# Last feed-forward of a two-block transformer kernel: first product by seven block products on halves of 256 tokens

## The reference, cut to what matters

```
D_FF_2 = 2816
def swiglu(h, w1, w2):
    a, b = jnp.split(h @ w1, 2, axis=-1)     # w1: 1024 x 5632
    return (jax.nn.silu(a) * b) @ w2         # w2: 2816 x 1024
def ffn_sublayer(x, m, i, g, w1, w2):
    return x + HALF_STEP * m[:, 3 * i + 2, None] * swiglu(mod_norm(x, m, i, g), w1, w2)
```

## Time and profile before

| | us |
|---|---|
| median of 3 runs | 3350.95 |
| lowest, highest | 3350.13, 3354.4 |
| profiled execution | 3347.27 |
| its span | 3345.5 |
| TensorE busy | 3238.1 (97%) |
| VectorE busy | 2444.6 (73%) |
| ScalarE busy | 1278.2 (38%) |
| GpSimd busy | 627.0 (19%) |

### The profile page before, as it was taken

The page is one execution under the profiler, slowest core; times in us unless marked ns, Lnnn a source line. Parts: engine busy times, 40 slices in busy tenths (PEclk is TensorE's granted clock), DMA queues, the critical chain, the costliest instruction groups (busy, mean ns, idle before and its releaser), DMA issues. The chain is left out here.

```text
span 3345.5 us, 45701 instructions
## 1 busy us (share of the span) xinstructions
PE 3238.1 (97%) x18042; PEld 2877.2 (86%) x18042; DVE 2444.6 (73%) x4483; ACT 1278.2 (38%) x2257; POOL 627.0 (19%) x657
## 2 busy tenths in 40 slices
PE   7989999999999999999999999999999999999998
PEld 6788778888999998877799999989999978788887
DVE  5576578888898898576788889888877865753333
ACT  4475543333332234345533333443333343533222
POOL 0100011112522221301052222143222213100000
PEclk9999999999999999999999999999999999999999
DMA  5201245554233333533213433322333243123332
GB/s 176 64 20 51 77 158 184 170 188 142 67 119 115 104 105 98 154 95 85 73 57 104 126 107 111 95 76 86 120 114 117 91 122 94 49 83 98 96 99 78
DMA packets 381928, 348.89 MB, mean 104 GB/s; under 512 B 17440, under 2 KB 338336, under 8 KB 381200
## 3 DMA queue, kind: packets, MB, share of 16 engines
q1 hardware_dynamic: 337696, 250.74, 24.8%
q0 software_dynamic: 17232, 46.84, 4.7%
q10 hardware_dynamic: 26784, 48.37, 4.5%
HBM read 339.60 MB, written 2.10 MB: 102 GB/s over the span
## 5 line engine op out<-in xcount | busy, mean ns | idle before, releaser
L824 PE MATMUL ps<-Hh,hib 128*128 128x512 f32 (+2 forms) x2672 | 955.9, 358 | 12.2 <-DVE Hl L2516 5.9
L824 PE MATMUL ps<-Hl,hib 128*128 128x512 f32 (+2 forms) x2672 | 946.0, 354 | 0.0
L824 PE MATMUL ps<-Hh,lob 128*128 128x512 f32 (+2 forms) x2672 | 945.7, 354 | 0.0
L1608 ACT ACTIVATE hib<-rawb 128x1024 fp32r<-128x1024 f32 (+2 forms) x589 | 508.9, 873 | 607.7 <-PE ps L824 606.8
L2381 DVE TENSOR_TENSOR lob<-rawb,hib 128x1024 fp32r<-128x1024 f32 (+2 forms) x361 | 441.4, 1226 | 383.7 <-ACT hib L1608 381.7
L824 PEld LDWEIGHTS ps<-Hh,hib 128*128 128x128 f32 x2672 | 507.8, 190 | 74.0 <-DVE Hl L2516 11.0
L824 PEld LDWEIGHTS ps<-Hh,lob 128*128 128x128 f32 x2672 | 507.6, 190 | 52.3
L824 PEld LDWEIGHTS ps<-Hl,hib 128*128 128x128 f32 x2672 | 508.3, 190 | 49.7 <-issue 1.0
L824 PE MATMUL ps<-Gha,hib 128*128 128x512 f32 (+1 forms) x704 | 238.0, 338 | 3.0 <-DVE lob L2381 1.9
L824 PE MATMUL ps<-Gla,hib 128*128 128x512 f32 (+1 forms) x704 | 237.3, 337 | 0.0
L824 PE MATMUL ps<-Gha,lob 128*128 128x512 f32 (+1 forms) x704 | 236.7, 336 | 0.0
(11 more groups left out here) (330 smaller groups left out, 5759.4 us busy)
## 6 DMA issues: line engine op xcount, KB each, us to landing
rawb<-in_ffn_w_in SPq DMA_DIRECT2D x114, 512.0 KB, 3.9
rawb<-in_ffn_w_out SPq DMA_DIRECT2D x76, 512.0 KB, 3.4
rawb<-in_w_in SPq DMA_DIRECT2D x74, 512.0 KB, 3.7
rawb<-in_w_ff SPq DMA_DIRECT2D x64, 512.0 KB, 3.8
rawb<-in_ffn_w_in SPq DMA_DIRECT2D x124, 256.0 KB, 3.3
MRa<-in_w_mod_t ACTq DMA_DIRECT2D x117, 256.0 KB, 3.3
MR<-in_w_mod_t POOLq DMA_DIRECT2D x112, 256.0 KB, 3.5
MRb<-in_w_mod_t ACTq DMA_DIRECT2D x59, 256.0 KB, 3.2
```

The costliest lines, as they stand in the source:

```text
L824: return e.matmul(out, lhsT, rhs, start=start, stop=stop)
L1608: return e.activation(out, src, f, **k)
```

## The change

Pairs 3 to 21 of the last feed-forward are computed by seven products, over halves of 256 tokens; pairs 0 to 2 stay plain. The parts are 3, 8 and 11 pairs, so the second product has three rounds of sweeps and not two. It has no seam there (`N != ("b", 1)`). The activation sums, their buffers and GpSimd's work are made for this feed-forward too. The matrix sizes of all others stay as they were.

```
-HALF = 384
+HALVES = {("a", 0): 384, ("b", 0): 384, ("a", 1): 384, ("b", 1): 256}
-def crossed(j, l):
-    return (j, l) != ("b", 1)
 def parts_of(j, l):
-    sizes = (PLAIN, 4, 4, 4, 3, 4) if crossed(j, l) else (11, 11)
+    sizes = (PLAIN, 8, 11) if (j, l) == ("b", 1) else (PLAIN, 4, 4, 4, 3, 4)
     return [(sum(sizes[:n]), sizes[n]) for n in range(len(sizes))]
...
             for f in range(f0, f0 + many):
-                if crossed(*name) and f >= PLAIN:
+                if f >= PLAIN:
                     cross((name, "in", f), w1, [128 * f, FF2 + 128 * f])
...
-                for n in "hl" if crossed(j, l) else "":
-                    sb(f"pad{n}{j}{l}", [128, 3, T + TC], where=s4)
-                    T2[j, l].append(sb(f"T{n}{j}{l}", [128, 2, HALF], where=s4))
+                for n in "hl":
+                    sb(f"pad{n}{j}{l}", [128, 2 * half * PLAIN], where=s4)
+                    T2[j, l].append(sb(f"T{n}{j}{l}", [128, 2, half], where=s4))
+                    if many > PLAIN + 1:
+                        sb(f"rest{n}{j}{l}", [128, 2 * half * (many - PLAIN - 1)], where=s4)
...
-        def acts_block(H_, b, q):
-            t0 = HALF * ((b - 1) // 2)
-            return H_[:, 2 * q + (b - 1) % 2, t0:t0 + HALF]
+        def acts_block(N, H_, b, q):
+            half = HALVES[N]
+            t0 = half * ((b - 1) // 2)
+            return H_[:, 2 * q + (b - 1) % 2, t0:t0 + half]
...
 (tensor: ffn)
-                        if crossed(*N) and f >= PLAIN:
+                        if f >= PLAIN:
                             seven(N, name)
...
                     residual((N, "out", part_), sets, ga, following(l, i) if part_ == len(parts) - 1 and len(sets) == 2 else None,
-                             crossed(*N))
+                             N != ("b", 1))
...
 (scalar: ffn)
-                if crossed(j, l):
-                    in_turn(grouped([lambda m=m, q=q: acts_sums(N, m, q) for m, q in SUMS], SUMS_BY))
+                in_turn(grouped([lambda m=m, q=q: acts_sums(N, m, q) for m, q in SUMS], SUMS_BY))
...
 (vector: ffn)
-                if crossed(j, l):
-                    in_turn(acts_sums(N))
+                in_turn(acts_sums(N))
...
 (gpsimd)
             def ffn(j, l, i):
                 N = (j, l)
-                name = {"x": xnorm(l, i), "c": cnorm(l, i)}
+                name = {"x": xnorm(l, i), "c": cnorm(l, i)} if (j, l) != ("b", 1) else {"x": xnorm(l, i)}
...
                 if l == 0:
                     load(mod_silu[TURNS["b", 0]], d["cc_rows"], "cc", TURNS["b", 0])
-                    ffn("b", l, 2)
+                ffn("b", l, 2)
                 fence(("b", l))
```

More of the change, by code:

```diff
@@ L620, in program @@
             for j in "ab":
-                many = max(n for _, n in parts_of(j, l))
+                many, half = max(n for _, n in parts_of(j, l)), HALVES[j, l]
                 s4 = ExitStack()
                 T2[j, l] = []
-                for n in "hl" if crossed(j, l) else "":
-                    sb(f"pad{n}{j}{l}", [128, 3, T + TC], where=s4)
-                    T2[j, l].append(sb(f"T{n}{j}{l}", [128, 2, HALF], where=s4))
+                for n in "hl":
[3 more added lines that the diff above has]
+                        sb(f"rest{n}{j}{l}", [128, 2 * half * (many - PLAIN - 1)], where=s4)
                 s4.close()
                 s4 = ExitStack()
-                G2[j, l] = [sb(f"G{n}{j}{l}", [128, many, T + TC], F32R, where=s4) for n in "hl"]
-                if crossed(j, l):
-                    E2[j, l] = [sb(f"E{n}{j}{l}", [128, 3, 4, HALF], F32R, where=s4) for n in "hl"]
-                    SUM2[j, l] = sb(f"SUM{j}{l}", [128, 3, 512], where=s4)
+                G2[j, l] = [sb(f"G{n}{j}{l}", [128, many, 2 * half], F32R, where=s4) for n in "hl"]
+                E2[j, l] = [sb(f"E{n}{j}{l}", [128, 3, 4, half], F32R, where=s4) for n in "hl"]
+                SUM2[j, l] = sb(f"SUM{j}{l}", [128, 3, 512], where=s4)
                 if (j, l) in TURNS:
@@ L722, in acts_sum @@
                 return E2[N][half][:, (5, 6, 7).index(m), q, :]
-            return acts_block(H_, 3 if m == 3 else ACTS[m][0], q)
+            return acts_block(N, H_, 3 if m == 3 else ACTS[m][0], q)
         def scratch(N, half, m, q):
@@ L730, in acts_operand @@
         def acts_operand(N, half, which, q):
-            return acts_sum(N, half, int(which), q) if isinstance(which, str) else acts_block((Hh, Hl)[half], which, q)
+            return acts_sum(N, half, int(which), q) if isinstance(which, str) else acts_block(N, (Hh, Hl)[half], which, q)
         def raw_of(c):
@@ L2116, in seven @@
             def seven(N, name, part, f, last):
+                half = HALVES[N]
                 def slot(which):
-                    return Tm[:, get("tmp", "seven", name, which)[0], 0:HALF]
+                    return Tm[:, get("tmp", "seven", name, which)[0], 0:half]
                 def gate(which):
@@ L2128, in high @@
                     w.wait_ge(*at("gfree", N, part - 1))
-                    act(G2[N][0][:, f, HALF * t:HALF * t + HALF], slot(which), ACT.Copy).then_inc(*done(("ghi", name, t)))
+                    act(G2[N][0][:, f, half * t:half * t + half], slot(which), ACT.Copy).then_inc(*done(("ghi", name, t)))
                 for pos, x in enumerate(P[name].units):
@@ L2141, in seven @@
                         w.wait_ge(*at("full", name, 1))
-                        act(slot("u"), ps[:, bank("o", name, 1), 0:HALF], ACT.Copy).then_inc(
+                        act(slot("u"), ps[:, bank("o", name, 1), 0:half], ACT.Copy).then_inc(
                             *done(("free", "o", name, 1), ("copied", name)))
@@ L2164, in ffn @@
                         name = (N, "in", f)
-                        if crossed(j, l) and f >= PLAIN:
+                        if f >= PLAIN:
                             seven(N, name, part, f - f0, f == f0 + many - 1)
@@ L3013, in seven @@
             def seven(N, name, part, f, last):
+                half = HALVES[N]
                 def slot(which):
-                    return Tm[:, get("tmp", "seven", name, which)[0], 0:HALF]
+                    return Tm[:, get("tmp", "seven", name, which)[0], 0:half]
                 def product(m):
                     w.wait_ge(*at("full", name, m))
-                    return ps[:, bank("o", name, m), 0:HALF]
+                    return ps[:, bank("o", name, m), 0:half]
                 def add(to, a, b, *keys, op=ALU.add):
@@ L3030, in low @@
                     w.wait_ge(*at("ghi", name, t))
-                    t0 = HALF * t
-                    e.tensor_tensor(G2[N][1][:, f, t0:t0 + HALF], slot(a), G2[N][0][:, f, t0:t0 + HALF], ALU.subtract).then_inc(
+                    t0 = half * t
+                    e.tensor_tensor(G2[N][1][:, f, t0:t0 + half], slot(a), G2[N][0][:, f, t0:t0 + half], ALU.subtract).then_inc(
                         *done(("tmp", "seven", name, a), *keys))
@@ L3425, in acts_sums @@
                     for k in (2 * q, 2 * q + 1):
-                        for s in "xc":
+                        for s in name:
                             w.wait_ge(*at("h", name[s], k))
```

6 lines of the change are left out of this document (3 added, 3 removed).

## The result

| | before | after |
|---|---|---|
| median, us | 3350.54 (4 runs, 3348.66 to 3354.4) | 3391.3 (4 runs, 3386.44 to 3392.23) |
| ratio, 95% interval | | 1.0117 (1.01 to 1.0135) |
| profiled execution, us | 3347.27 | 3392.23 |
| its span, us | 3345.5 | 3390.4 |

The changed kernel is slower by 1.2%, some 41 us. The forecast was 3354.0 with a range up to 3372; the time lies outside it, beyond the rival on VectorE's queue (3375) too.

What follows compares the result with a forecast made beforehand. A loop through the raw weight buffers, 11.5 us a pair, was taken to bound the pairs by seven; -15.2 + 12.9 + 1.6 + 0.4 + 2.5 + 0.8 = +3.0 us gave 3354.0 us, range 3342 to 3372.

Steps and rivals of the forecast that it cites:

- rival on VectorE's queue: Pairs by seven: VectorE's in-order queue sets the pace, 12.3 us a pair; +24 us, 3375; chance 0.18.
- matmuls, 19 x 0.80: TensorE, 19 pairs: 10.08 us by seven products against 10.88 plain, saving 0.80 a pair, 15.2 us.
- waiting in the two parts: Parts of 8 and 11: TensorE waits as pairs fall behind from the third on, 4.3 + 8.6 = 12.9 us.
- three plain pairs: Opening plain pairs: activation sums delay the fifth weight chunk, TensorE waits 1.6 us (0 to 4).
- round for the part of 3, clock included: Second product, part of 3: 2.5 us waiting for the third pair's G, plus 0.8 for lower clock.
- norm: Final norm: GpSimd's first two sums meet its last steps on SBUF operands, 0.4 us (0 to 1).
- a loop through the raw weight buffers: Pairs by seven: fourth sum, load and next three sums set 11.5 us a pair (10.8 to 12.2); chance 0.62 with the stalls.
- VectorE's own need: VectorE in a pair by seven: 11.0 us, scaled from 12.3 at 384 columns, above TensorE's 10.08.
- second rival: Pairs by seven: VectorE's queue decides, including 1.3 us of unhidden waits, less 2 x 4 done ahead; 3375, chance 0.18.
- The remark on the fourth sum: GpSimd's fourth sum: its 3.84 us wait for VectorE's low halves left out, as these come earlier at 256 columns.
- third rival: TensorE's clock: waits of 1.5 us in every pair bring it down, five falls of 1.7 us; +11.5, 3362; chance 0.06.
- The place of the waits: Last pairs of each part: TensorE would wait at m=6, behind a low half of SUM.

Runs made afterwards that it cites:

- e_nosum: Changed kernel with GpSimd's four weight sums in the last feed-forward cut to 8 of 128 columns, part of the computation left out; ratio to before 0.9996.
- e_sum4: Changed kernel with two places in turn for the fourth sum of weights in the last feed-forward; ratio to before 1.0117, stage 398.2 us.
- e_raw4: Changed kernel with a fourth raw weight buffer from the last plain pair of the last feed-forward on; ratio to before 1.0125, stage 402.2 us.
- e_both: Changed kernel with interleaved first sweeps in the part of 3, two places for the fourth sum and a fourth raw buffer; ratio to before 1.0141, stage 407.9 us.
- e_seam: Changed kernel with the two first sweeps of the part of 3 interleaved; ratio to before 1.0117, stage 399.4 us.
- e_fulld: Changed kernel with second gating one product later, interleaved first sweeps, fourth raw buffer and two places for the fourth sum; median 3380.72 us, ratio to before 1.0101.
- e_defer: Changed kernel with each pair's second gating and what hangs on it one product later on VectorE and ScalarE; median 3372.8 us, ratio to before 1.0072.

## Why the prediction was wrong

| step | predicted, us | measured, us |
|---|---|---|
| matmuls, 19 x 0.80 | -15.2 | -15.2 at the pace of 0.120 (e_nosum, 10.1 a pair) |
| waiting in the two parts | +12.9 | +47.3 |
| three plain pairs | +1.6 | +1.6 |
| round for the part of 3, clock included | +3.3 | +8.4 |
| other rounds | 0 | +0.3 |
| norm | +0.4 | not separable from where the stage starts |
| sum | +3.0 | +42.5 on the stage |

**The step that failed** is the one that set what bounds a pair: "the tighter thing is a loop through the raw weight buffers", 11.5 us. Of 42.5 us on the stage, freeing one of its buffers took 5.1 or 1.1 (e_sum4, e_raw4), and freeing both, with the seam, added 4.6 (e_both). What binds is VectorE's queue, with what it loses beside GpSimd's sums and waiting for ScalarE. It was already in the loop that I read from the earlier trace rows. The 1.65 us from the end of the fourth sum (2635.37) to the load (2637.02) I took for a fixed step of SyncE's, but the load went out 0.03 us behind a low half of VectorE's (start us, us; kernel before):

```profile
2636.31 0.68 DVE L2383 TENSOR_TENSOR lob<-rawb,hib 128x512 fp32r<-128x512 f32 x1
```

So did every load of the changed kernel's part of 11. Nor was the loop's range all above a plain pair's 10.88, as the prediction says: its lower end was 10.8.

VectorE's own need I had at 11.0 us from "12.3 - 11 x 0.12" and put aside as below the loop. It was 12.2: 8.0 us of work and 4.2 of standing behind GpSimd's sums (e_nosum beside the changed kernel). The subtraction is right for the work, but it keeps the standing as it was at 384 columns. In four pairs there (2087.30 to 2145.40) the operations with both inputs in SBUF lasted 9.5 us longer than 0.68 and 0.548 us each, 2.4 a pair:

```profile
L2383 DVE TENSOR_TENSOR lob<-rawb,hib 128x512 fp32r<-128x512 f32 x14 | 16.6, 1193 | 0.7 <-ACT hib L1608 0.6
...
L3023 DVE TENSOR_TENSOR Tm<-Tm 128x384 f32<-128x384 f32 x7 | 4.9, 694 | 0.1
L3032 DVE TENSOR_TENSOR Glb<-Tm,Ghb 128x384 fp32r<-128x384 f32 x6 | 4.6, 762 | 0.0
```

In the pair shown above it is 3.9, so the same four sums held VectorE up for some 1.5 us more. To this comes the time in which VectorE waits for ScalarE behind its own gating, 1.43 us a pair, which I had only in the second rival, as 1.3. The second rival had the mechanism and the right side, and its 12.3 us was too small for a pair at 13.6; its slack of 4 us in each part was too small the other way (11 x 13.61 - 139.0 = 10.7 in the part of 11).

**The remark on the fourth sum failed too.** I let its 3.84 us of waiting in the earlier trace rows go, since those low halves "hang on TensorE's pace and come earlier at 256 columns". They hang on VectorE's queue, and the fourth sum still waits 2.3 us in eleven of the 19 pairs and 0.1 to 0.9 in the others.

**A term was left out.** At the start of the second product after a part by seven, TensorE waits 1.6 us for the first weight chunk's low half: 2 x 1.6 = 3.2 of the 47.3 (L2380 in the list of waits).

**The part of 3.** Its place was right, the third pair's G behind the sum m = 3. It was mis-sized: 5.3 us of waiting for 2.5, and for the clock 3.0 for 0.8 (4 us at 0.50 and 6 at 0.83, 2.0 + 1.0 lost). By these shares TensorE ran for 6 us at half clock; the third rival's 1.7 us for such a fall and the 3.4 us at half clock in the expectation of e_seam were too low. I had only the chain of one pair, and not the low half and the addition in front of it in VectorE's queue.

**What was right.** The pace of the matmuls, and that the first pairs of a part keep 10.1 us. The plain stage's 1.6 came out in part by luck: the wait was 0.9 us, and 0.4 of the rest lies in the first pair, ahead of that wait. The place of the waits was wrong: I had them in front of product 6, behind its sum, and they are in front of 4, 3 and 1. In the part of 11 the first pairs took 27.22 us for 2.7 pairs' matmuls with no wait at all; such a stretch by itself would have borne out the forecast, and the loss comes only after it.

The third rival, the clock, held in one place only: 0.50 after the gap of 5.3 us. In the parts by seven, with waits of up to 1.7 us in every pair from the third on, the granted clock stayed at 1.00.

Open is why e_raw4 and e_sum4 by themselves differ by 4 us. VectorE is busy for 47.5 us in four pairs of the one and 45.6 in four of the other (3220.00 to 3273.24, 3220.57 to 3272.15), which is the right size, but why its operations meet the sums differently was not followed up.

## What to carry to other kernels

Where VectorE and GpSimd share a stage, split VectorE's busy time into work and time behind GpSimd, by comparing the mean of the same operation with and without a sum beside it; only the first part scales with the tile, and the second has to be reckoned anew (2.4 us a pair at 384 columns, 3.9 here). On an engine that runs in order the waits inside its queue cost as much as its work, so moving a gating and what hangs on it back in two queues (-20 us on the stage) can be worth more than two more buffers (+5 us, the seam's gain in it). Before a gap between two events is taken for a latency, see what ended it. And when a cheaper method loads a helper engine, use it for as many steps as that engine can follow, with the old method between them.

## What the runs showed of the hardware that I had not expected

- Freed buffers can cost time: the fourth sum started earlier and cost VectorE 0.86 us a pair that the wait had hidden (e_fulld beside e_defer; read from the traces, not isolated).
- A load on SyncE's queue follows what releases it closely: 0.03 us behind VectorE's low half, in the earlier trace rows and throughout the part of 11.
- GpSimd's sums hardly suffer in this meeting: 1.30, 1.35 and 1.62 us with VectorE operations beside them, 1.28 to 1.71 in the earlier trace rows, though one of the 76 in the changed kernel took 2.15. It is VectorE that stands, three operations in a row. No run shows a full sum with VectorE quiet.
- Short waits cost TensorE more than their length as the profile counts it: in the pair of 13.61 us three waits leave it busy for 10.85 us on matmuls that take 10.08 without a break.
